# The fourth pair's down weights in a fused hybrid layer with 32 experts: issued after the first gather has landed, or without that wait

## The chip, the cores and the metric

The kernel runs on one core of one Trainium2 chip. The metric is the device time of one execution in microseconds, lower is better. All data are float32 in HBM.

## What is computed

One decoder layer on 512 tokens of width 1024: a combined input projection feeds a state space branch and an attention branch, their outputs pass one output projection and are added to the input. Then every token goes to two of 32 gated experts. The change touches only the second half:

```python
def hierarchical_moe(x, w_rg, b_rg, w_re, b_re, w_gate, w_up, w_down):
    """x: (b,s,D). Top-1 expert group, then top-2 experts within that group."""
    ...
    def per_seq(args):
        xi, gi = args
        hid = jax.nn.silu(jnp.einsum('sd,edf->sef', xi, w_gate)) * jnp.einsum('sd,edf->sef', xi, w_up)
        return jnp.einsum('sef,se,efd->sd', hid, gi, w_down)
```

Each expert has a gate and an up matrix of 1024 x 256 and a down matrix of 256 x 1024, 3 MB together and 96 MB for all 32.

## The kernel before

The order of all work is written out by hand, one program per engine, tied by semaphores. Three stages follow each other: the input projection in passes over blocks of 512 columns, the mixers with the output projection, and the experts.

**The experts' stage** works on `NPAIR` = 16 pairs of experts (e and e + 16), each with at most `CAP` = 64 tokens, in the two halves of the 128 partitions. For pair p the steps are:

- GpSimd gathers the token rows from `x2_rows` in HBM into the buffer `xg` (`gather(p)`, line 678, an indirect DMA that increments `xg_in0` or `xg_in1`); its indices are `slot_rows`, made at line 1944.
- TensorE transposes them (line 1446), ScalarE and VectorE copy the result to `xgT` (lines 1007 and 1973).
- TensorE multiplies by the gate and up weights in `gu{p % 3}` (line 1461) and increments `gate_up_done`; ScalarE and VectorE form `hid` (lines 1014 and 1980), which TensorE transposes (line 1470).
- TensorE multiplies by the down weights in `dn{p % 4}` (line 1485) and increments `down_done`; ScalarE and VectorE scale the rows (lines 1020 and 1993), and GpSimd adds them to `out` with an indirect DMA (line 689).

TensorE's program is a pipeline. It begins with the transposes of pair 0, its gate and up products and the transposes of pair 1; after that it goes pair by pair.

**The weights** are all issued by SyncE, in the order of its program: `load_gate_up` (line 366, four DMAs of 1 MB a pair) and `load_down` (line 382, two DMAs of 1 MB a pair). All of them go to one hardware queue of 16 rings; gathers and additions by GpSimd go to another (the software queue). There are three gate and up buffers and four down buffers. The weights of pair 0 and most of those of pairs 1 and 2 are issued while the output projection still runs. Then SyncE stores the four chunks of the layer's middle result `zs` twice, to `x2_rows` (line 475, `x2_out`) and to `out` (line 476, `out_stored`), and issues the rest of the weights of pairs 1 and 2. The next instruction is the load of the fourth pair's down weights, `load_down(sp, 3, 3)`, 2 MB. Its buffer `dn3` lies over `zs`, so it needs the stores out of `zs`, the squares and the transposes of `zs` to be over (lines 482 to 485). Behind it stands `load_gate_up(sp, 3, 0)`, which waits for the first `gate_up_done`, since buffer `gu0` is then free.

Of the kernel before, what the change touches and what calls it, by code (L numbers as in the profile page):

```python
# [81 lines left out]
def hybrid_layer(nc, x, norm_mix_w, w_in, conv_w, conv_b, dt_bias, a_log, d_skip, ssm_norm_w, q_norm_w, k_norm_w,  # L82
# [7 lines left out]
    with ExitStack() as ctx:  # L90
# [17 lines left out]
        def sem(name):  # L108
            if name not in sems:
                sems[name] = ctx.enter_context(nc.semaphore(name))  # L110
            return sems[name]
# [49 lines left out]
        sp, lf, cum, tot, ncum, ecum, dte, etot = (m[n] for n in ("sp", "lf", "cum", "tot", "ncum", "ecum", "dte", "etot"))  # L161
# [196 lines left out]
        def load_gate_up(sp, p, b, wrap=False, parts=(0, 1, 2, 3)):  # L358

            e = p % NPAIR if wrap else p  # L360
            for half in range(2):
                for which, w in ((0, w_expert_gate), (1, w_expert_up)):
                    if 2 * half + which not in parts:
                        continue
                    src = w[0][bass.ds(e + half * NPAIR, 1)].rearrange("e (p k) f -> p (e k f)", p=P)
                    sp.dma_start(m[f"gu{b}"][:, half, which, :, :].rearrange("p k f -> p (k f)"), src).then_inc(sem(f"gu_in{b}"), 16)  # L366
# [30 lines left out]
        def _(sp):  # L397
# [79 lines left out]
            sp.wait_ge(sem("pass_done"), N_END)  # L477
            load_gate_up(sp, 1, 1, parts=(1,))
            load_gate_up(sp, 2, 2, parts=(0, 1))
            sp.wait_ge(sem("xg_in0"), 16)  # L480

            sp.wait_ge(sem("x2_out"), 16 * TC)
            sp.wait_ge(sem("out_stored"), 16 * TC)
            sp.wait_ge(sem("f_squared"), TC)
# [1553 lines left out]
```

## Time and profile before

| | us |
|---|---|
| median of three timed runs | 779.5 (777.0 to 781.03) |
| the profiled execution | 777.04 |
| its span in the profile | 775.4 |
| TensorE busy | 707.5 (91%) |
| VectorE busy | 380.5 (49%) |
| ScalarE busy | 278.9 (36%) |
| GpSimd busy | 145.5 (19%) |

The profile gives all times from the start of the span. A busy share is an average over stages with different limits; the DMA share, which is no engine's, stands in slices of the span beside them.

### The profile page before, as it was taken

The page shows a single profiled execution, that of the slowest core. Times are in us where ns is not written, and L with a number is a line of the kernel's source. Part 1 is how long each engine was busy: PE and PEld are TensorE (multiplying, and loading weights), DVE is VectorE, ACT ScalarE, POOL GpSimd, SP SyncE. Part 2 cuts the span into 40 slices and gives each one's busy share as a digit, 9 for nine tenths or more (in the row PEclk, how much of TensorE's full clock was granted, in tenths as well). Part 3 has the DMA queues.
Part 4 walks back from the last instruction along what each step waited for, and adds up shares of the span by engine and source line. Part 5 has one row for each costly group of instructions (what it writes and reads, how often), then busy time and mean ns, then how long its engine had stood idle before and what let it go on. Part 6 is the DMA issues. An engine that isn't in the chain of part 4 may idle for free.

```text
span 775.4 us, 10367 instructions
## 1 busy us (share of the span) xinstructions
PE 707.5 (91%) x3828; PEld 471.1 (61%) x3828; DVE 380.5 (49%) x758; ACT 278.9 (36%) x647; POOL 145.5 (19%) x126
## 2 busy tenths in 40 slices
PE   6999999999999999999999999978999686968784
PEld 5867888788888888666566688863433232323221
DVE  6876877775877733766776543570211111111100
ACT  4934633544454445544554333212211111211100
POOL 3513331330311102000210032011122111111111
PEclk9999999999999999999999999968999798989988
DMA  8333212330303221600110079786999999999972
GB/s 277 84 109 109 94 43 90 101 95 14 109 10 101 66 90 63 218 1 1 55 56 1 1 269 423 292 347 274 398 399 408 394 409 413 407 412 406 387 284 43
DMA packets 44038, 150.31 MB, mean 194 GB/s; under 512 B 11557, under 2 KB 11649, under 8 KB 32209
## 3 DMA queue, kind: packets, MB, share of 16 engines
q1 hardware_dynamic: 38384, 134.61, 45.4%
q0 software_dynamic: 4720, 8.70, 4.5%
q10 hardware_dynamic: 880, 6.30, 2.1%
q8 instruction: 33, 0.54, 0.3%
q14 instruction: 21, 0.16, 0.1%
HBM read 145.09 MB, written 12.88 MB: 204 GB/s over the span
## 4 chain that ended last, share of the span: by engine, by line
PE 69%; SPq 13%; DVE 6%; DMA 6%; ACT 3%; issue 2%; POOL 0%; POOLq 0%; ACTq 0%; DVEq 0%
PE bank L1083 13%; PE bank L1085 12%; PE bank L1084 12%; PE bank L1461 9%; SPq L366 9%; SPq L382 4%; DMA s_gu<-in_w_expert_up_dram 4%; PE bank L1485 4%; PE bank L1320 3%; PE bank L1292 2%; PE bank L1306 2%; DVE s_wl L260 2%; PE bank L1200 2%; PE bank L1296 1%; DMA s_raw<-in_w_in_dram 1%
## 5 line engine op out<-in xcount | busy, mean ns | idle before, releaser
L1461 PE MATMUL bank<-s_gu,s_xgT 128*64 128x512 f32 x512 | 125.7, 648 | 34.9 <-DMA s_gu<-in_w_expert_up_dram 31.6
L1461 PEld LDWEIGHTS bank<-s_gu,s_xgT 128*64 128x64 f32 x512 | 42.5, 149 | 115.9 <-issue 112.1
L260 DVE TENSOR_TENSOR s_wl<-s_raw,s_wh 128x512 fp32r<-128x512 f32 x84 | 88.6, 1093 | 25.6 <-ACT s_wh L763 25.1
L763 ACT ACTIVATE s_wh<-s_raw 128x512 fp32r<-128x512 f32 x120 | 74.0, 630 | 40.9 <-PE bank L1085 18.4
L1083 PE MATMUL bank<-s_wh,s_hTh 128*128 128x512 f32 x192 | 78.7, 410 | 0.0
L260 POOL TENSOR_TENSOR s_wl<-s_raw,s_wh 128x512 fp32r<-128x512 f32 x36 | 53.6, 1503 | 131.5 <-ACT s_wh L763 131.1
L1085 PE MATMUL bank<-s_wh,s_hTl 128*128 128x512 f32 x192 | 75.0, 391 | 0.0
L1084 PE MATMUL bank<-s_wl,s_hTh 128*128 128x512 f32 x192 | 74.8, 390 | 0.0
L1987 DVE COPY s_hidT<-bank 128x256 f32<-128x256 f32 x16 | 6.8, 424 | 118.3 <-PE bank L1470 118.3
L1485 PE MATMUL bank<-s_dn,s_hidT 128*64 128x512 f32 x256 | 58.5, 598 | 1.0 <-DVE s_hidT L1987 1.0
L1014 ACT ACTIVATE s_sg<-bank,s_slot_scale 128x256 f32<-128x256 f32 x16 | 7.6, 473 | 138.1 <-PE bank L1461 138.1
L917 ACT ACTIVATE s_Pe<-bank,s_nmax 128x128 f32<-128x128 f32 (+3 forms) x64 | 33.6, 526 | 53.7 <-DVE s_nmax L1784 53.7
L689 POOL DMA_INDIRECT out_dram<-s_yrow,s_slot_rows x16 | 25.2, 1576 | 86.0 <-DVE s_yrow L1993 68.6
L1084 PEld LDWEIGHTS bank<-s_wl,s_hTh 128*128 128x128 f32 x192 | 36.1, 188 | 8.3 <-issue 1.4
L1083 PEld LDWEIGHTS bank<-s_wh,s_hTh 128*128 128x128 f32 x192 | 36.1, 188 | 8.2 <-issue 1.4
L1085 PEld LDWEIGHTS bank<-s_wh,s_hTl 128*128 128x128 f32 x192 | 36.0, 188 | 7.8
L678 POOL DMA_INDIRECT s_xg<-x_rows,s_slot_rows x16 | 16.6, 1037 | 126.6 <-PE bank L1446 123.1
L1083 PE MATMUL bank<-s_hTh,s_wh 128*128 128x512 f32 x96 | 38.4, 400 | 0.0
L1085 PE MATMUL bank<-s_hTh,s_wl 128*128 128x512 f32 x96 | 37.5, 391 | 0.0
L1084 PE MATMUL bank<-s_hTl,s_wh 128*128 128x512 f32 x96 | 37.4, 390 | 0.0
L1993 DVE TENSOR_SCALAR s_yrow<-bank,s_slot_scale 128x512 f32<-128x512 f32 x16 | 12.0, 751 | 48.2 <-PE bank L1485 48.2
L1485 PEld LDWEIGHTS bank<-s_dn,s_hidT 128*64 128x64 f32 x256 | 17.0, 136 | 30.5 <-issue 27.4
(277 smaller groups left out, 1308.7 us busy)
## 6 DMA issues: line engine op xcount, KB each, us to landing
s_dn<-in_w_expert_down_dram SPq DMA_DIRECT2D x30, 1024.0 KB, 24.7
s_gu<-in_w_expert_gate_dram SPq DMA_DIRECT2D x28, 1024.0 KB
s_gu<-in_w_expert_up_dram SPq DMA_DIRECT2D x28, 1024.0 KB
s_raw<-in_w_in_dram SPq DMA_DIRECT2D x88, 256.0 KB, 3.4
s_raw<-in_w_out_dram SPq DMA_DIRECT2D x32, 256.0 KB, 3.4
s_xin<-in_x_dram SPq DMA_DIRECT2D x4, 512.0 KB, 6.1
s_zs<-in_x_dram SPq DMA_DIRECT2D x1, 2048.0 KB, 10.3
s_gu<-in_w_expert_gate_dram ACTq DMA_DIRECT2D x2, 1024.0 KB
```

What stands on the lines that cost most here:

```text
L260: eng.tensor_tensor(low, full, high.bitcast(F32), ALU.subtract).then_inc(sem(f"{what}_low_{low_engine(what, i)}"), 1)
L366: sp.dma_start(m[f"gu{b}"][:, half, which, :, :].rearrange("p k f -> p (k f)"), src).then_inc(sem(f"gu_in{b}"), 16)
L382: sp.dma_start(m[f"dn{b}"][:, half, :, :].rearrange("p k n -> p (k n)"), src).then_inc(sem(f"dn_in{b}"), 16)
L689: pool.indirect_dma_start(out=out[:, :], out_offset=bass.IndirectOffsetOnAxis(ap=slot_rows[:, p:p + 1], axis=0), in_=m["yrow"][:, j, :], i ...
L763: act.activation(wh[:, i % HL, :], raw[:, i % RAW, :], ACT.Copy).then_inc(sem("w_high"), 1)
L917: act.activation(Pe[:, v % 3, 0:n], ps[4 + v % 3][:, 0:n], ACT.Exp, bias=nmax[:, v:v + 1], accum_out=rsum[:, v:v + 1]).then_inc(sem("p_exp ...
L1083: pe.matmul(dst, ah, bh, start=start, stop=False)
L1084: pe.matmul(dst, ah, bl, start=False, stop=False)
L1085: return pe.matmul(dst, al, bh, start=False, stop=stop)
L1320: last = pe.matmul(ps[7][par * HD:(par + 1) * HD, qb * P:(qb + 1) * P], V[:, kb, h * HD:(h + 1) * HD], PT[:, par, kb * P:(kb + 1) * P], st ...
L1461: last = pe.matmul(ps[j][r, :].rearrange("p (w f) -> p w f", w=2), m["xgT"][:, j, k, r], gu[:, half, :, k, :], start=(k == 0), stop=(k == ...
L1485: last = pe.matmul(ps[6 + nb][r, :], m["hidT"][:, j, at:at + CAP], dn[:, half, q, nb * BLK:(nb + 1) * BLK], start=(q == 0), stop=(q == 1))
```

## The change

One wait is taken out of SyncE's program. The first gather (pair 0, into `xg`) increments `xg_in0` when it lands. Before, SyncE waits for that ahead of the four waits that protect `zs`, and only then issues the fourth pair's down weights.

```diff
             load_gate_up(sp, 1, 1, parts=(1,))
             load_gate_up(sp, 2, 2, parts=(0, 1))
-            sp.wait_ge(sem("xg_in0"), 16)
-
             sp.wait_ge(sem("x2_out"), 16 * TC)
             sp.wait_ge(sem("out_stored"), 16 * TC)
             sp.wait_ge(sem("f_squared"), TC)
             sp.wait_ge(sem("x2_transposed"), 2 * TC)
             load_down(sp, 3, 3)
             sp.wait_ge(sem("gate_up_done"), 1)
             load_gate_up(sp, 3, 0)
```

SyncE's instructions at this place, with before's rows marked - and the changed kernel's +. `s_dn` is the down weights' buffer, `s_gu` the gate and up weights'; the two rows ahead are the last loads for pair 2:

```order
 L366 DMA s_gu<-in_w_expert_gate_dram 128x2048
 L366 DMA s_gu<-in_w_expert_up_dram 128x2048
-L382 DMA s_dn<-in_w_expert_down_dram 128x2048 [waits f_squared,out_stored,x2_transposed,x2_out,xg_in0]
+L382 DMA s_dn<-in_w_expert_down_dram 128x2048 [waits f_squared,x2_transposed,out_stored,x2_out]
 L382 DMA s_dn<-in_w_expert_down_dram 128x2048
 L366 DMA s_gu<-in_w_expert_gate_dram 128x2048 [waits gate_up_done]
```

The order of the instructions is the same; one name is gone from the list of what the first down load waits for.

## Rows read from the trace of the kernel before

**Rows 1.** The page, part 2: clock, DMA share and rate in 40 slices.
```profile
PEclk9999999999999999999999999968999798989988
DMA  8333212330303221600110079786999999999972
GB/s 277 84 109 109 94 43 90 101 95 14 109 10 101 66 90 63 218 1 1 55 56 1 1 269 423 292 347 274 398 399 408 394 409 413 407 412 406 387 284 43
```
**Rows 2.** The chain that ended last, in time: start us, us, what.
```profile
516.41 0.61 DVE s_pick L1941
517.35 0.58 issue
518.16 3.80 DMA s_xg<-x_rows,s_slot_rows
522.00 1.99 PE bank L1446 x8
524.01 1.15 ACT s_xgT L1007 x4
525.20 8.80 PE bank L1461 x32
534.07 1.28 ACT L1014
...
537.06 7.09 PE bank L1461 x32
...
604.64 3.61 PE bank L1485 x16
608.25 0.63 SPq L382
...
707.25 30.33 DMA s_gu<-in_w_expert_up_dram
737.58 0.14 issue
737.72 10.04 PE bank L1461 x32
```
**Rows 3.** SyncE's waits over the span: who waited for whom, us, times, longest.
```profile
SPq L366 <- PE bank L1461: 37.4, 5, 11.2
...
SPq L382 <- DMA s_xg<-x_rows,s_slot_rows: 7.9, 1, 7.9
...
SPq L484 <- DMA out_dram<-s_zs: 2.8, 1, 2.8
```
**Rows 4.** SyncE's DMA issues in time: start us, us, line, operation.
```profile
509.49 1.62 SPq L366 DMA_DIRECT2D s_gu<-in_w_expert_up_dram  x1
521.97 0.80 SPq L382 DMA_DIRECT2D s_dn<-in_w_expert_down_dram  x2
534.02 0.33 SPq L366 DMA_DIRECT2D s_gu<-in_w_expert_gate_dram  x1
```
**Rows 5.** TensorE's timeline: start us, us, line, operation, idle before and its releaser.
```profile
522.00 1.97 PE L1446 MATMUL bank<-s_ident,s_xg 128*128 128x128 f32 x8 [0.95 <-DMA s_xg<-x_rows,s_slot_rows]
525.20 8.77 PE L1461 MATMUL bank<-s_gu,s_xgT 128*64 128x512 f32 x32 [1.23 <-ACT s_xgT L1007]
533.91 1.16 PE L1446 MATMUL bank<-s_ident,s_xg 128*128 128x128 f32 x8
```
**Rows 6.** Windows: engines' busy us (instructions), then clock, DMA share, GB/s.
```profile
518.00:519.00 1.00, 1.00 (x6) 1.00 (x5) 0.83 (x4) 0.00 (x0) 0.84 (x1) 0.50 0.82 344
519.00:520.00 1.00, 1.00 (x17) 0.94 (x19) 0.00 (x0) 0.00 (x0) 0.69 (x2) 0.50 0.33 139
525.00:528.60 3.60, 3.40 (x8) 1.00 (x10) 0.00 (x0) 0.15 (x1) 0.79 (x1) 0.50 0.99 412
529.00:530.00 1.00, 1.00 (x8) 0.33 (x6) 0.00 (x0) 0.00 (x0) 0.00 (x0) 1.00 0.36 127
530.00:540.00 10.00, 8.01 (x42) 3.30 (x40) 1.08 (x2) 2.79 (x6) 0.99 (x1) 1.00 0.50 188
540.00:550.00 10.00, 10.00 (x52) 4.23 (x50) 2.26 (x4) 2.30 (x6) 0.99 (x1) 1.00 1.01 411
615.00:616.00 1.00, 0.53 (x2) 0.33 (x4) 0.00 (x0) 0.00 (x0) 0.00 (x0) 0.50 1.00 328
620.00:621.00 1.00, 1.00 (x5) 0.28 (x3) 0.00 (x0) 0.00 (x0) 0.00 (x0) 0.60 0.98 401
```
**Rows 7.** The gathers (line 678), singly and all 16: issue to landing, us.
```profile
L678 POOL DMA_INDIRECT s_xg<-x_rows,s_slot_rows x1: 1147/1147/1147, 518.2 to 518.2; - x1
DMA to landing us min/median/max: 3.8/3.8/3.8
...
L678 POOL DMA_INDIRECT s_xg<-x_rows,s_slot_rows x1: 988/988/988, 524.8 to 524.8; - x1
DMA to landing us min/median/max: 6.4/6.4/6.4
...
L678 POOL DMA_INDIRECT s_xg<-x_rows,s_slot_rows x1: 1043/1043/1043, 662.2 to 662.2; - x1
DMA to landing us min/median/max: 8.0/8.0/8.0
...
DMA to landing us min/median/max: 3.6/8.4/9.7
```
**Rows 8.** DMA queues: packets, MB, share of 16 engines; from 518:525, then 524:530.
```profile
q0 software_dynamic: 288, 0.46, 22.8%
...
q1 hardware_dynamic: 264, 1.90, 76.4%
```

## Prediction

> **What bounds the kernel now.** I read the slices first [rows 1]. In the last two fifths of the span the DMA engines are at nine tenths or more and move about 400 GB/s, so the experts' stage should be a stream of weights with TensorE beside it. One slice in that stretch stands out with six tenths, near 530 us. The chain of waits in order of time [rows 2] tells how the stage begins: the token indices are made, the first gather takes 3.80 us from 518.16, the transposes begin at 522.00, the copies at 524.01, the gate and up products of pair 0 at 525.20. TensorE has stood idle for 0.95 us when the gather lands [rows 5], so the gather's landing is on the path at this point, with nothing else that comes near it. [...]
>
> The windows [rows 6] say which of the two really sets the end. Between 530 and 540 us the DMA share is 0.50: the fourth pair's down weights are in, and the next load, the gate and up weights of pair 3, may only be issued when buffer 0 is free. SyncE issues it at 534.02 [rows 4], when the products of pair 0 are over. From 540 us on the share is 1.01, and the page shows nine tenths in every slice up to the last two. So from about 535 us on the time is that of a fixed list of transfers, one behind the other, and a fixed tail of products behind the last. What matters is **when that list starts**. It starts when TensorE has done pair 0, and that hangs on the first gather.
>
> **The change, part by part.** One wait goes. It cost SyncE 7.9 us, behind a wait of 2.8 us for the last store out of the middle result [rows 3]. SyncE's issue before them ends at 511.11 [rows 4], so the store has landed at 511.11 + 2.8 = 513.9 us. The other three conditions are older: they concern the same chunk's first store, squares and transposes, and no wait of SyncE for them is in the list. The 2 MB of down weights are therefore issued at 513.9 instead of 521.97 us, 8.0 us sooner.
>
> What is this worth? Nobody waits for these weights: pair 3 multiplies by them two pairs and more after pair 1, and they are in by 530. The instruction behind them in SyncE's program waits for the end of pair 0's products, whose time doesn't come from SyncE. The transfers after 535 us are the same in number. **The gain is zero**; the idle stretch of the DMA engines, now 530 to 535 us, only moves ahead and grows, since it still ends when pair 0 is done. Only if that end came sooner would there be a gain.
>
> What does it cost? At 518.16 the first gather is issued. Now the DMA engines are finishing the loads of pair 2 then (share 0.82 in the window from 518, 0.33 in the next [rows 6]), and the gather has them nearly for itself. After the change 2 MB stand in the other queue: 2.10 MB at the 412 GB/s of the window from 525 [rows 6] are 5.1 us. Begun at 518.9 they would last to 524.0, and with the gather's own share to 524.8: both first gathers take 22.8% of 7 us of all engines [rows 8], 1.6 us, half of it for one. The whole gather runs beside the weights.
>
> What a gather costs then is read from the others [rows 7]: 3.8 us for this one, 6.4 for that of pair 2, which was issued at 524.80 into the same 2 MB but saw them end about 529.4 (the share falls to 0.36 in the window from 529 [rows 6]), and 8.0 as the lowest of those under full load, with a median of 8.4 over all 16 and 9.7 at most. The gather of pair 2 landed at 531.2, 1.8 us after its load had ended. Ours would have its load until 524.8, so by that reckoning it lands at 526.6, 8.4 us after its issue, which is also the median. I take **8.0 us**, the lowest value under full load, since here the load ends just as the gather does. The bounds are 6.3 and 9.7, and 3.8 if the queue ahead should not matter at all.
>
> That is 8.0 - 3.8 = 4.2 us on the path. The transposes, copies and products behind it keep their durations, buffer 0 comes free 4.2 us later, at 538.2, and the list of transfers starts 4.2 us later. The second gather, next in GpSimd's program, lands later too, but its transposes stand behind pair 0's products at 533.91 [rows 5] and at 538.1 afterwards: hidden, and it would cost only if it took over 15 us more.
>
> A small term is the clock. TensorE runs at half speed, 1.2 GHz, in the window 525.00 to 528.60 and at 2.4 GHz after it, 3.4 us after the products began [rows 6]. In another place of this trace, where the engine had been idle since 608.25 [rows 2] and began products at 615.5 (busy for 0.53 us of the window 615 to 616), the window 620 to 621 has a mean of 0.60, so full speed came at 620.8, after 5.3 us [rows 6]. The longer idle time ahead of pair 0 could stretch 3.4 us to 5.3. An added us at half speed loses half a us of work, so this is 0 to 1.0 us. I take 0, the row of the same place.
>
> **Sum.** Profiled execution 777.04 (span 775.4) + 4.2 = 781.2 us. The median of the runs shown is 779.5, 2.5 above the profiled one, so on the median's scale 779.5 + 4.2 = **783.7 us**, 0.54% slower.
>
> **The rivals.**
>
> *Turns between the queues (782.0 us).* A gather has 288 / 2 / 16 = 9 packets on each DMA engine, and a packet of weights holds an engine for 76.4% of 6 us x 16 / 264 = 0.28 us [rows 8]. If each packet of the gather waits for one of weights and no more, that is 9 x 0.28 = 2.5 us: landing after 6.3, time 779.5 + 2.5 = 782.0. The 6.4 us of pair 2's gather speak for it, the sixteen's median of 8.4 against it, since a gather under full load should not take longer than that rule gives. The Trainium skill ("DMA: Bandwidth & Descriptors", section "Queues, rings and completion order") has each DMA engine go round between its queues packet by packet, which is this rival; the full-load rows lie 2 us above what it would give. The same section says that a completion write lands after all earlier writes of its engine, across queues, which could be part of these 2 us; no row here shows it apart.
>
> *Not slower (779.5 to 780.8, or 777.8).* The gather pays little because its 0.46 MB for two are small and its descriptors are taken up while the loads of pair 2 end. It has even now 0.82 of load in its first us and lands after 3.8. Then the path keeps its time. If, beside that, the clock rose before the products of pair 0 began, they would take 7.1 us like those of pair 1 (the chain has 7.09 for pair 1 and 8.80 for pair 0 [rows 2], 1.7 more) and the whole comes out at 779.5 - 1.7 = 777.8. This decides if the gather's delay is below 1.7 us. Against it: not one gather after the second landed under 6.4 us.
>
> *The weights are not issued sooner (779.5).* If another of the four conditions held SyncE until 520 us or so, nothing would change. The 2.8 us row names the store, and the 7.9 us row only the gather; I give this 3 in 100.
>
> **How the numbers follow.** The forecast (landing after 7.5 to 9.7 us, +3.7 to +5.9, with the clock's term up to +6.9) has 0.57. Turns between queues 0.21. Not slower 0.19, with the 0.03 of the unchanged issue 0.22 together. A measurement of this kernel can tell about 0.5% from no change, which is 3.9 us, so the forecast straddles that line: about four fifths of its 0.57 lie above, 0.46, and 0.02 come from the turns with a late clock. Slower 0.48. Faster by 3.9 us has no mechanism in these rows, since nothing before 535 us can be shortened by more than 1.7 us; I leave 0.05 for what I don't see. The rest, 0.47, is the same. The range reaches up to 779.5 + 5.9 + 1.0 = 786.4, and down to 779.6, so that only a part of the "not slower" case is left out, and the small chance above.
>
> **What the changed kernel's profile would show.** The down weights issued at about 513.9; SyncE's wait for the gather gone and its wait for line 1461 longer by 12 us; the first gather 8 us to landing (6.3: turns; 4: no cost); TensorE's wait ahead of the first transposes 5 us instead of 0.95; the gate and up load of pair 3 issued about 538; an idle stretch of the DMA engines from about 526 to 539; behind it the same shift of 4.2 us at every pair and in the chain's last wait. The prediction is wrong if the shift at 534 us isn't found at the end: then transfers after 535 are not a fixed list. It is wrong in its main term if the gather lands below 7.5 us.

## The result and the profile after

The median of six runs of the changed kernel is 783.04 us (778.59 to 783.54), against 778.03 us for six runs of before. The ratio is 1.0046, with a 95% interval of 1.0025 to 1.0067: the change makes the kernel **slower by 3.6 us** (1.9 to 5.2). The two medians differ by more, 5.0 us. A second series of seven runs gave 1.0059 (1.0037 to 1.0082).

The page of the changed kernel, part 2, beside [rows 1]:

```profile
PEclk9999999999999999999999999968999798989998
DMA  8333212320303221600110079793999999999982
GB/s 277 84 109 109 94 49 88 97 94 14 109 15 95 76 85 57 217 1 1 55 56 1 1 287 422 294 410 135 406 410 395 395 415 406 406 412 407 392 312 46
```

The two slices that had 8 and 6 tenths of DMA share near 530 us have 9 and 3 now. The same bytes have moved ahead, and the hole behind them is deeper.

SyncE's waits and issues, beside [rows 3] and [rows 4]. Lines below the change have numbers smaller by two:

```profile
SPq L366 <- PE bank L1459: 50.6, 6, 23.4
...
SPq L483 <- DMA out_dram<-s_zs: 2.5, 1, 2.5
```
```profile
509.50 1.12 SPq L366 DMA_DIRECT2D s_gu<-in_w_expert_up_dram  x1
513.26 0.97 SPq L382 DMA_DIRECT2D s_dn<-in_w_expert_down_dram  x2
537.60 0.33 SPq L366 DMA_DIRECT2D s_gu<-in_w_expert_gate_dram  x1
```

The wait for the gather is gone, the down weights are issued at 513.26 instead of 521.97 us, and SyncE stands 23.4 instead of 11.2 us before pair 3's gate and up load. That load comes at 537.60 instead of 534.02. What SyncE no longer waits for the gather it waits for the products, and the load still goes out 3.6 us later.

The chain in time, beside [rows 2]:

```profile
517.88 8.02 DMA s_xg<-x_rows,s_slot_rows
525.95 1.98 PE bank L1444 x8
527.95 1.15 ACT s_xgT L1005 x4
529.14 8.44 PE bank L1459 x32
...
710.03 30.57 DMA s_gu<-in_w_expert_up_dram
740.59 0.14 issue
740.73 8.44 PE bank L1459 x32
```

The first gather takes 8.02 us where it took 3.80. Where these 4.2 us go is told by the packets of the two queues. First before from 518 to 520 and from 520 to 522 us, then the changed kernel from 518 to 522 and from 522 to 526 us (packets, MB, share of 16 engines; q0 is the gathers' queue, q1 the weights'):

```profile
q1 hardware_dynamic: 74, 0.48, 57.6%
...
q0 software_dynamic: 189, 0.34, 63.2%
```
```profile
q1 hardware_dynamic: 237, 1.71, 101.6%
...
q0 software_dynamic: 281, 0.46, 30.1%
```

In before the gather's first packet runs at 520.0, 1.9 us after its issue at 518.16. In the changed kernel none runs before 522.3, 4.4 us after the issue at 517.88, while the weights keep every engine busy. So 2.5 of the 4.2 us pass before the gather has moved a byte, and 1.7 us are lost between its first packet and its landing (3.6 us there, 1.9 in before), where its packets run among those of the weights. The transposes and copies behind it keep their durations. The products of pair 0 begin 3.9 us later; the wait at the end of the list of transfers ends 3.0 us later (740.59 against 737.58). These products belong to pair 14. They took 10.04 us in before and 8.44 here, and that is why this profiled execution is only 1.6 us longer in its span (777.0 against 775.4). The reason is the clock. Before's window and then the changed kernel's, columns as in [rows 6]:

```profile
741.00:743.00 2.00, 2.00 (x8) 0.67 (x6) 0.00 (x0) 0.00 (x0) 0.00 (x0) 0.50 1.03 371
743.00:745.00 2.00, 2.00 (x11) 0.61 (x9) 0.00 (x0) 0.00 (x0) 0.00 (x0) 0.83 1.10 258
```
```profile
739.00:741.00 2.00, 0.27 (x2) 0.30 (x4) 0.00 (x0) 0.00 (x0) 0.00 (x0) 0.77 1.00 399
743.00:745.00 2.00, 2.00 (x10) 0.70 (x8) 0.00 (x0) 0.00 (x0) 0.00 (x0) 0.88 1.01 412
```

The means put the return of full speed at 743.7 us in before, 6.0 us into the products, which began at 737.72 at half speed. In the changed kernel it came at 743.5, 2.8 us into the products. One execution's span can't show an effect of 4 us to better than this.

The windows around pair 0 in the changed kernel:

```profile
524.00:525.00 1.00, 0.00 (x0) 0.00 (x0) 0.00 (x0) 0.00 (x0) 0.00 (x0) 0.50 0.80 308
525.00:526.00 1.00, 0.06 (x1) 0.06 (x1) 0.00 (x0) 0.00 (x0) 0.00 (x0) 0.50 0.36 135
...
530.00:540.00 10.00, 8.64 (x40) 3.18 (x36) 0.55 (x2) 2.34 (x5) 0.58 (x1) 0.91 0.25 68
```

The first gather lands at 525.90 us, and from about then the DMA engines stand almost idle till 538.

### The profile page after: what moved, and what is told of

The parts are those of the page before. It is cut to its first block, busy times and chain, and to the rows that moved or that the text cites. A ratio compares the mean times of both kernels' runs of the same rounds, so it can differ in the third digit from the quotient of the medians.

```text
span 777.0 us, 10367 instructions
## 1 busy us (share of the span) xinstructions
PE 705.6 (91%) x3828; PEld 470.1 (61%) x3828; DVE 380.4 (49%) x758; ACT 278.8 (36%) x647; POOL 145.6 (19%) x126
## 4 chain that ended last, share of the span: by engine, by line
PE 66%; SPq 15%; DMA 6%; DVE 6%; ACT 3%; issue 2%; POOL 0%; POOLq 0%; ACTq 0%; DVEq 0%
PE bank L1081 13%; PE bank L1083 12%; PE bank L1082 12%; SPq L366 10%; PE bank L1459 8%; SPq L382 4%; DMA s_gu<-in_w_expert_up_dram 4%; PE bank L1483 3%; PE bank L1318 3%; PE bank L1290 2%; PE bank L1304 2%; DVE s_wl L260 2%; PE bank L1198 2%; PE bank L1294 1%; DMA s_raw<-in_w_in_dram 1%
## 5 line engine op out<-in xcount | busy, mean ns | idle before, releaser
L1459 PE MATMUL bank<-s_gu,s_xgT 128*64 128x512 f32 x512 | 124.1, 641 | 34.2 <-DMA s_gu<-in_w_expert_up_dram 31.0
## 6 DMA issues: line engine op xcount, KB each, us to landing
s_gu<-in_w_expert_up_dram SPq DMA_DIRECT2D x28, 1024.0 KB, 26.4
```

The source lines that it names most:

```text
L1459: last = pe.matmul(ps[j][r, :].rearrange("p (w f) -> p w f", w=2), m["xgT"][:, j, k, r], gu[:, half, :, k, :], start=(k == 0), stop=(k == ...
```

## The experiments

The profiled executions start the experts' stage at different times: the first gather is issued between 517.8 and 522.0 us, which is not the change's doing: it is 517.8 to 522.0 in the kernels without early down weights and 517.9 to 520.0 in those with them. So the traces are compared from that issue, g. In the table the columns from the third to the sixth are us after g, the last is the sixth less the fifth. "Load of pair 3" and "of pair 4" are the issues of the first of their gate and up DMAs, "list ends" is where the products of pair 14 begin, after the last big wait of the chain.

| kernel | g | gather lands | load of pair 3 | load of pair 4 | list ends | last less pair 4 |
|---|---|---|---|---|---|---|
| before | 518.16 | 3.8 | 15.9 | 26.0 | 219.6 | 193.6 |
| changed | 517.88 | 8.0 | 19.7 | 29.9 | 222.9 | 193.0 |
| changed, again | 519.97 | 7.9 | 21.3 | 31.5 | 225.0 | 193.5 |
| half of the down weights early | 518.76 | 6.3 | 18.5 | 28.7 | 222.2 | 193.5 |
| early in small pieces | 519.62 | 6.7 | 18.7 | 28.9 | 222.2 | 193.3 |
| down weights late | 520.49 | 4.7 | 17.6 | 26.8 | 224.9 | 198.1 |
| before, load cut in two | 522.03 | 3.9 | 12.8 | 26.4 | 219.2 | 192.9 |
| before, load cut in three | 518.67 | 4.0 | 10.9 | 26.2 | 219.2 | 193.0 |
| changed, load cut in two | 518.14 | 8.3 | 18.0 | 31.6 | 224.5 | 192.9 |
| before, both gathers waited for | 517.76 | 3.7 | 15.7 | 25.8 | 218.9 | 193.1 |
| before, cut and transposes moved | 518.62 | 3.8 | 12.2 | 23.8 | 216.6 | 192.9 |
| before, transposes moved | 519.89 | 3.9 | 17.5 | 24.3 | 220.1 | 195.8 |
| changed, cut, transposes moved | 518.50 | 8.3 | 18.3 | 29.8 | 222.6 | 192.8 |
| before, cut, moved, both gathers waited for | 518.68 | 3.8 | 12.4 | 24.0 | 216.9 | 193.0 |

### The changed kernel again

No edit. The question was whether the short profiled execution or the longer timed runs are the usual case.

> The changed kernel a second time, unaltered, to see whether its profiled execution (span 777.0 us, 1.6 above that of before) or its timed runs (4 to 5 us above) is the usual case. Theory (the first gather is delayed by about 4 us and all transfers behind pair 0 start that much later): ratio to before 1.004 to 1.006, first gather 8.0 us to landing, pair 3's gate and up load issued 3.6 to 4.2 us later than before. Rival (the delay is mostly regained later in the stage): median within 2 us of before.

Measured: 783.1 us, ratio 1.0059 (1.0037 to 1.0082). The gather again takes 7.9 us, but pair 3's load comes 5.4 us later after g than in before, not 3.6 to 4.2. The rest is pair 0's products, 10.08 us instead of 8.77, because the clock came back later:

```profile
531.15 10.08 PE L1459 MATMUL bank<-s_gu,s_xgT 128*64 128x512 f32 x32 [1.23 <-ACT s_xgT L1005]
```
```profile
531.00:537.00 6.00, 5.85 (x14) 1.72 (x16) 0.00 (x0) 0.10 (x1) 0.73 (x1) 0.50 0.19 49
537.00:538.00 1.00, 1.00 (x6) 0.30 (x4) 0.00 (x0) 0.00 (x0) 0.00 (x0) 0.90 0.00 0
```

Half speed lasted until 537.2, 6.0 us into the products, where it had lasted 3.4 us in before [rows 6] and 2.7 us in the first trace of the changed kernel, whose window has a mean of 0.58:

```profile
531.00:532.00 1.00, 1.00 (x6) 0.33 (x4) 0.00 (x0) 0.00 (x0) 0.00 (x0) 0.58 0.50 176
```

So in these two executions the clock moved the result by -0.4 and +1.3 us against before's. The rival, that the delay is regained later in the stage, is out: the timed runs keep it.

### Half of the down weights early

```diff
-            load_down(sp, 3, 3)
+            load_down_half(sp, 3, 3, 0)
+            sp.wait_ge(sem("xg_in0"), 16)
+            load_down_half(sp, 3, 3, 1)
```

> Half of the fourth pair's down weights (1 MB) issued early, the other half after the first gather has landed. Theory A (the gather is held for as long as the weights ahead of it flow, plus about 1.8 us): the load ends about 521.9 us, landing 5.4 to 6.0 us after issue, products of pair 0 about 2 us later than before, time +1.5 to +2.2 us. Theory B (any queue ahead costs the full-load latency): landing 7.5 to 8.5 us, time as the changed kernel. Theory C (turns, one packet of weights for each of the gather's 9): as long as the 1 MB lasts, landing about 5.8 to 6.3.

Measured: landing after 6.3 us, ratio 1.0040 (1.0025 to 1.0055).

The queue of the weights from 518.8 to 521.8 us:

```profile
q1 hardware_dynamic: 176, 1.30, 102.8%
```

The gather's first packet runs at 521.9, 3.1 us after its issue (1.9 in before, 4.4 in the changed kernel), and from 523.5 on hardly a packet of the weights is left; the gather lands at 525.1. Half the bytes gave 2.5 of the 4.2 us, 1.3 of them ahead of the first packet: the price grows with the bytes ahead, and theory B (any queue ahead costs the full price) is out. Theories A and C gave nearly the same number for this run; 6.3 is a little above what A said and the upper end of C, and neither has a wait ahead of the gather's first packet. The timed cost, 3.1 us (1.9 to 4.3), is larger than the 1.5 to 2.2 expected; the profile has +2.6 at the list's end.

### The early down weights in small pieces

```diff
+                for q in range(4):
+                    last = sp.dma_start(m[f"dn{b}"][:, half, :, :].rearrange("p k n -> p (k n)")[:, q * cols:(q + 1) * cols],
+                                        src[:, q * cols:(q + 1) * cols])
```

> The changed kernel with the fourth pair's down weights in eight DMAs of 256 KB, 2 KB of each partition at a time, in place of two of 1 MB with 8 KB. All 2 MB stay ahead of the first gather. If the delay comes from turns between the queues packet by packet, it shrinks with the packet: 9 packets x 0.07 to 0.14 us, landing after 4.5 to 5.5 us, time about +1 us over before. If it comes from the bytes ahead, whatever their packets, landing stays at 7.5 to 8.5 us and the time at +4.

Measured: 6.7 us to landing, 780.52 us, ratio 1.0038 (1.0018 to 1.0059). Neither side is right: 1.3 us less than with the large pieces, yet 2.9 more than without weights. Here the gather landed at 526.3, while the engines were still full:

```profile
526.00:527.00 1.00, 0.65 (x3) 0.65 (x4) 0.00 (x0) 0.00 (x0) 0.00 (x0) 0.50 1.02 369
527.00:528.00 1.00, 1.00 (x7) 0.92 (x5) 0.00 (x0) 0.00 (x0) 0.00 (x0) 0.50 0.47 176
```

So a gather need not wait for the queue ahead to run dry. The weights' queue from 519.6 to 524 us, and the gathers' queue from 524 to 527 us:

```profile
q1 hardware_dynamic: 733, 1.75, 101.1%
...
q0 software_dynamic: 278, 0.46, 42.7%
```

The first packet of the gather runs at 524.1, 4.5 us after its issue, no sooner than with the large pieces. From there to the landing it takes 2.2 us, where it took 3.6 with the large pieces and 1.9 in before. So the size of the pieces sets what the gather loses once its packets run, as the rival of turns says (1.7 us with large pieces, 0.3 with small, in one trace each), and doesn't touch the 2.5 us before. Turns alone therefore don't account for the delay: by the rival's own sum a wait of 0.28 us for each of 9 packets makes 6.3 us, and 8.0 were measured with large pieces. Why the first packet waits longer with 2 MB ahead, whatever their pieces, no run shows. The same wait stands in before where the engines are full: the gather issued at 546.25 has its first packet at 550.4 and lands after 8.5 us.

### The down weights late

```diff
-            load_down(sp, 3, 3)
             sp.wait_ge(sem("gate_up_done"), 1)
+            load_down(sp, 3, 3)
             load_gate_up(sp, 3, 0)
```

> The fourth pair's down weights issued after the first gate_up_done, just ahead of pair 3's gate and up load, so that they are 2.1 MB more in the list of transfers that starts there, while nothing disturbs pair 0. If transfers behind pair 0 are a fixed list at full rate: 2.1 MB / 0.41 MB per us = +5.1 us over before (784 us or so), with the first gather at 3.8 us to landing. If that list has slack somewhere, less: within 2 us of before.

Measured: 782.33 us, ratio 1.0050 (1.0030 to 1.0069), which is 3.9 us. The list's end lies 198.1 us behind the issue of pair 4's load where it is 193 in the others: the 2.1 MB cost their full 5 us in this column. The gather landed after 4.7 us instead of the 3.8 expected, although no down weights were in flight and its first packet ran 1.9 us after its issue as in before. Why the rest took 2.9 us instead of 1.9 isn't known; so much can come without weights ahead. The chain's last wait and what it released:

```profile
714.64 30.65 DMA s_gu<-in_w_expert_up_dram
745.29 0.14 issue
745.42 9.38 PE bank L1459 x32
```

So the idle stretch behind the gather is worth the whole transfer: before's place fills it, this one doesn't, and the two differ by 3.9 us in time and 5.4 at the list's end, of which 0.8 come from the later gather (the load of pair 4 is at 26.8 instead of 26.0).

### Pair 3's load cut in two, on before

The load's first half of the rows is let go when pair 0 has used them.

```diff
+            for part, (a, b) in enumerate([(0, 4), (4, 8)]):
+                if part < 1:
+                    sp.wait_ge(sem("gu0_used"), part + 1)
+                else:
+                    sp.wait_ge(sem("gate_up_done"), 1)
...
+                    if isinstance(p, int) and p == 0 and k + 1 in (4, 0):
+                        last.then_inc(sem("gu0_used"), 1)
```

> The kernel before with pair 3's gate and up load cut in two by rows: the first half of the rows (k 0 to 3) is issued when pair 0 has done its products with them, the second at gate_up_done. If the time hangs on when the transfers behind pair 0 start, the first half issues 16 products sooner, about 530.3 instead of 534.0 us, the idle stretch of the DMA engines shrinks by 3.7 us, and the time falls by about 3.5 us (ratio 0.9955). If the end is set otherwise: same.

Measured: 777.4 us, ratio 0.9981 (0.9967 to 0.9994), which is 1.5 us instead of 3.5. The load went out 3.1 us sooner after g, as meant, and the list ended 0.3 us sooner. The rest was lost here:

```profile
547.00:548.00 1.00, 1.00 (x8) 0.21 (x3) 0.00 (x0) 0.00 (x0) 0.00 (x0) 1.00 0.75 307
548.00:549.00 1.00, 1.00 (x8) 0.73 (x7) 0.18 (x1) 0.47 (x1) 0.00 (x0) 1.00 0.27 111
549.00:550.00 1.00, 1.00 (x9) 0.68 (x9) 0.92 (x3) 0.29 (x2) 0.00 (x0) 1.00 0.86 131
```
```profile
534.79 0.33 SPq L392 DMA_DIRECT2D s_gu<-in_w_expert_gate_dram  x1
...
548.38 0.33 SPq L369 DMA_DIRECT2D s_gu<-in_w_expert_gate_dram  x1
```

Pair 3's weights are in at about 548, and the next load, pair 4's, waits for the products of pair 1, which are over at 548.3. The hole has only moved from pair 0 to pair 1. The cut load was slower besides: from 540 to 543 us it moved 303 to 320 GB/s at a DMA share of 0.94 to 1.01, where before's uncut load moved about 400. The prediction's "fixed list of transfers" from about 535 us on was wrong in this direction: it can't start sooner than pair 4's load lets it. Of the 1.5 us of time the trace accounts for 0.3; this kernel, the one cut in three and the one with both gathers waited for were timed in one series and came out at 777.4, 777.3 and 777.3 us, against 778.63 for before there and 777.48 to 778.1 in the other series, so a part of it may be scatter.

### Cut in three, on before

```diff
-            for part, (a, b) in enumerate([(0, 4), (4, 8)]):
+            for part, (a, b) in enumerate([(0, 2), (2, 4), (4, 8)]):
```

> The same with three parts, rows k 0 and 1, 2 and 3, 4 to 7. The first issues 24 products sooner, about 528.7 us, while the fourth pair's down weights still flow, so that the DMA engines need not stop: time 4.5 to 5.5 us below before, if rows of 2 KB in the first two parts cost no rate. Rival: short rows and eight more issues on SyncE eat the gain, same as the two parts.

Measured: ratio 0.9990 (0.9975 to 1.0006), list's end at 219.2, as with two parts. The 5.0 us by which pair 3's load went out sooner bought nothing more, as the rival said. Its reason, the short rows, isn't told apart from pair 4's load, which is at 26.2 and has the list end 193.0 us behind it. The transfers were slow, with the engines full. A window, and the hardware queue's row (packets, MB, share) from 533 to 538 us:

```profile
538.00:539.00 1.00, 1.00 (x6) 0.34 (x4) 0.00 (x0) 0.00 (x0) 0.00 (x0) 1.00 0.98 213
```
```profile
q1 hardware_dynamic: 742, 1.36, 93.9%
```

From 533 to 538 us a packet carries 1.8 KB (1.36 MB / 742), and the engines move 1.36 MB in 5 us, 272 GB/s. In the window from 538 the last part's packets of 4 KB run among them, and it is slower still.

### Cut in two, on the changed kernel

The same edit on the changed kernel.

> The changed kernel with pair 3's gate and up load cut in two as in the run on before. The gather is still delayed by about 4 us, the list of transfers starts about 4 us sooner than in the changed kernel: time within 1 us of before. If the early down weights had any use once the list starts sooner, it would come out below the cut kernel made from before; the theory says 4 us above it.

Measured: 781.95 us, ratio 1.0050 (1.0031 to 1.0070), 4.6 us above the cut kernel made from before. The 4 us between the two were expected; "within 1 us of before" was not met, for the same reason as in the run on before: the cut gains little while pair 4's load holds the list, and pair 4's load stands behind the gather too (31.6 us after g).

### Both first gathers waited for, on before

```diff
             sp.wait_ge(sem("xg_in0"), 16)
+            sp.wait_ge(sem("xg_in1"), 16)
```

> The kernel before with one wait more: the fourth pair's down weights are issued after both first gathers have landed. They then flow about 1.5 us later, still ahead of pair 3's load. Theory (their time is free as long as they are over before the list behind pair 0 starts): same as before, within 0.5 us, first gather 3.8 us to landing. Rival (the transfers near pair 0 are not free): 1 us or more slower.

Measured: ratio 0.9980 (0.9965 to 0.9994). The rival of a cost is out. A gain of 1.6 us wasn't expected; after g, the list ends 0.6 us sooner than in before (one trace each). The last run below puts it to a test.

### Cut, and pair 1's transposes inside pair 0's products

If the list's end follows pair 4's load, what has to come sooner is pair 1's products. In before TensorE waits between the two pairs for pair 1's copies, which stand behind pair 0's SiLU. The edit, on the kernel with the cut load:

```diff
+                    if isinstance(p, int) and p == 0 and k == 5:
+                        tokens_transpose(1, 1)
...
             gate_up(0, 0)
-            tokens_transpose(1, 1)
...
+            tokens_copy(1, 1)
             gate(0, 0, slot_scale[:, 1, 0:1])
-            tokens_copy(1, 1)
```

The last three lines stand for ScalarE; VectorE's copies and its product of pair 0 change places in the same way.

> The kernel before with the cut load of pair 3 and, new, pair 1's transposes moved into pair 0's products (after k = 5), its copies ahead of pair 0's SiLU, so that pair 1's products follow pair 0's with no gap. Revised theory (the end follows the start of pair 1's products, since the release of pair 4's load hangs on them, 200.0 to 200.7 us before the last big wait ends): pair 1's products start 2 to 2.5 us earlier after the first gather's issue than the 18.9 us of before, last wait and time 1.5 to 2.5 us below before (ratio 0.997 to 0.998). Old theory (only the start of pair 3's load counts): as the cut load alone, 0.998 or more.

Measured: 776.11 us, ratio 0.9974 (0.9959 to 0.9990), 2.0 us below before.

```profile
525.71 6.82 PE L1476 MATMUL bank<-s_gu,s_xgT 128*64 128x512 f32 x24 [1.23 <-ACT s_xgT L1022]
532.46 1.16 PE L1461 MATMUL bank<-s_ident,s_xg 128*128 128x128 f32 x8
533.55 8.80 PE L1476 MATMUL bank<-s_gu,s_xgT 128*64 128x512 f32 x40
```
```profile
541.00:550.00 9.00, 9.00 (x48) 3.61 (x46) 2.25 (x4) 2.30 (x6) 2.00 (x2) 1.00 1.03 425
```

The time alone doesn't separate this kernel from the one with the cut alone (0.9981, 0.9967 to 0.9994); the traces do. The 40 products in one row are pair 0's last eight and all of pair 1's, with no gap. Pair 4's load goes out 2.2 us sooner after g, the DMA engines are full from 541 to 550, and the list ends 2.9 us sooner.

### The transposes moved, the load whole

> The same transposes and copies moved, but pair 3's load whole, at gate_up_done, which comes about 1 us later for the transposes now in front of it. Revised theory: pair 3's 4 MB then bound the list (they start 1 us later, and last 10 us), pair 4's load has no gap before it; time within 1 us of before, against 1.5 to 2.5 us gained with the cut load. If the cut is not needed: as the run with both.

Measured: 780.47 us, ratio 1.0025 (1.0012 to 1.0039), 2.0 us **above** before: a miss of the "within 1 us". Pair 4's load is early (24.3), but pair 3's comes 1.6 us later than in before (17.5), since the transposes now stand ahead of the release of buffer 0, and then its 4 MB fill the engines past pair 4's issue:

```profile
537.35 0.33 SPq L366 DMA_DIRECT2D s_gu<-in_w_expert_gate_dram  x1
...
544.21 0.33 SPq L366 DMA_DIRECT2D s_gu<-in_w_expert_gate_dram  x1
```

This is the one kernel, beside the one with late down weights, in which the last column isn't 193: the list hangs on pair 3's load here, 202.7 us ahead of its end (203.1 to 203.7 in the uncut kernels). By the list's end the cut alone gains 0.3 us, the transposes alone lose 0.6, and together they gain 2.9.

### Both edits on the changed kernel, and with both gathers waited for

> Both edits on the changed kernel. The first gather stays at 8.0 us to landing, so everything is 4 us later than in the run on before: 1.5 to 2.5 us below the changed kernel, 3.5 to 4.5 us above the run on before with both edits (ratio to before about 1.002 to 1.004).

Measured: 779.61 us, ratio 1.0023 (1.0011 to 1.0034), 3.5 us above the same edits on before. The early down weights cost about their 4 us in this arrangement also. The list's ends of the two traces lie 6.0 us apart (222.6 and 216.6): 4.5 of them are the gather's landing, and 1.5 the first 24 products of pair 0, which took 8.36 us instead of 6.82.

> The two edits on before, with the fourth pair's down weights held until both first gathers have landed. If that hold gained something by itself (its run alone came out at 0.998 of before, where the same was expected), this is 1 to 1.5 us below the run with the two edits; if that was chance, the same as it within 0.5 us.

Measured: 776.21 us, ratio 0.9969 (0.9953 to 0.9985), within 0.5 us of the run with the two edits (776.11 us, 0.9974). Holding the down weights for the second gather gains nothing that these runs can show; the 0.9980 of its own run is most likely the scatter between series, which remains unproven. The fastest kernels are these two, 2.0 to 2.4 us below before.

## Why the prediction was right, point by point

**The gain of zero.** Right. The down weights went out at 513.26 (513.9 predicted), 8.7 us sooner, and nobody had waited for them. SyncE took the time as a longer wait, 23.4 us, 12.2 more (12 predicted).

**The first gather's price.** Right: 8.0 us to landing predicted, 8.0 and 7.9 measured. The half load (6.3) and the small pieces (6.7) show that the weights ahead are the cause, the more bytes the more, and in part by the size of their pieces. That the number came out at 8.0 rests on the rows of other gathers under full load, not on a mechanism: the prediction counted from the end of the load (1.8 us after it), while here 2.5 of the 4.2 us passed before the first packet, and with small pieces the gather landed while the engines were still full. TensorE's wait ahead of the first transposes was to be 5 us and is 5.17:

```profile
525.95 1.97 PE L1444 MATMUL bank<-s_ident,s_xg 128*128 128x128 f32 x8 [5.17 <-DMA s_xg<-x_rows,s_slot_rows]
```

**The rival of turns** (landing after 6.3, 782.0 us) lies 1.7 us too low for the landing. Its sum has nothing for the time ahead of the first packet, where 2.5 us went, and 2.5 us for the turns, where 1.7 went; the trace disagrees with the rule as I applied it. I also took a packet of the profile, 8 KB of one partition, for the packet of the Trainium skill ("DMA: Bandwidth & Descriptors", section "Queues, rings and completion order"), which holds several descriptors, typically 9 to 17; whether they are the same no run shows. The run with small pieces does give the turns a part: the order of packets matters, not only that of bytes. The same section's other sentence, on a completion write that waits for earlier writes of its engine, is not tested by these runs.

**The clock's term.** Taken as 0, bounded by 0 and 1.0. It was -0.4 in the first trace and +1.3 in the second: the bound was too narrow on both sides. And it appears a second time, at pair 14's products (8.4 to 10.1 us over the traces), which the prediction left out. In the first pair of traces the two places together gave back 2.0 us, which is why the profiled executions differed by 1.6 us only; that was chance.

**The way to the end.** The prediction said that a shift of pair 3's load is found unaltered at the end. For a delay it holds within half a us or so: +3.9 at pair 3's load and +3.3 at the list's end in the first trace, +5.4 and +5.4 in the second. As a general statement it is wrong, and the cut loads show the step: the list of transfers hangs on the later of two releases, pair 3's load + 203 us and pair 4's load + 193 us. In before the two are within 1 us of each other (15.9 + 203 and 26.0 + 193), so a delay of the gather moves both, and a gain at pair 3 alone stops at the other. The forecast for the change didn't hang on this, since a delay moves both releases by the same amount.

**The sum.** +4.2 us predicted; +3.6 (1.9 to 5.2) and +4.6 (2.9 to 6.4) measured in the two series, 783.04 and 783.1 us against 783.7. The two last numbers are nearer than they deserve: 783.7 starts from before's median of three runs, 779.5, and before's longer series have 778.03 and 777.48, from which the medians are 5.0 and 5.6 us up. By the first ratio the result lies just inside the half per cent that the text called no change, by the second outside it; the forecast straddled that line and said so.

## What to carry to other kernels

A transfer that nobody waits for isn't free while a small one on the path shares its engines: ask what is in flight when the next needed bytes are issued, and put the bulk behind them if there is idle room later. Here the room of 5 us behind the gather took the bulk at no cost that a run shows. Before an early start of a stream is counted as a gain, look for the next release in the stream: two buffers that come free one behind the other can both be the bound, and moving one gains little at the end (0.3 us here, 2.9 with both).

## What the runs showed of the hardware

- An indirect gather of 0.23 MB by GpSimd (0.46 for two [rows 8]) took 3.6 to 4.7 us from issue to landing with few weights in flight, 6.3 us with 1 MB ahead, 7.9 to 8.3 us with 2 MB ahead, and 6.7 us when the 2 MB came in pieces of 2 KB a partition instead of 8 KB. Its first packet ran 1.9 us after the issue without early down weights, 3.1 with 1 MB, 4.4 with 2 MB and 4.5 with 2 MB in small pieces; from there to the landing it took 1.9 (2.9 in the kernel with late down weights), 3.2, 3.6 and 2.2 us. The small pieces shortened the second part and not the first.
- Pair 3's gate and up weights cut in three moved 272 GB/s from 533 to 538 us at a share of 93.9%, with packets of 1.8 KB, and 213 in the window behind it at 0.98, where uncut loads move about 400. The down weights in small pieces had packets of nearly the same size and moved 381 to 401 in the windows from 521 to 524 us, at a share of 0.98 to 1.05. Why the two differ was not tried.
- TensorE came back to full speed 2.7 and 6.0 us after pair 0's products began, in two executions of the same kernel with nearly the same idle time ahead of them (5.2 and 5.1 us before the transposes). The products took 8.41 and 10.08 us.
